# One-hot rows for the first expert block, a fixed expert order, row scaling on ScalarE and a resident norm row

## What is computed

```python
hn = rmsnorm(h, norm_ffn_w)
g_sel = argmax(hn @ router_group_w + b)                # one of 4 groups
top_l, top_i = top_k(e_logits of that group, 2)        # two of its 8 experts
weights = p_group * softmax(top_l)
ys = (silu(xb @ w_gate[e]) * (xb @ w_up[e])) @ w_down[e]   # per block of tokens of one expert
h = h + segment_sum(ys * buf_w, buf_tok)
out = rmsnorm(h, final_norm_w)
```

## Time and profile before

| | |
|---|---|
| median of 3 runs | 2898.2 us (2897.41 to 2901.9) |
| profiled execution | 2901.05 us |
| its span, first to last instruction | 2899.3 us |
| TensorE busy | 2523.1 us (87%) |
| VectorE busy | 917.7 us (32%) |
| ScalarE busy | 776.6 us (27%) |
| GpSimd busy | 171.6 us (6%) |
| DMA | 610.93 MB, mean 211 GB/s |

### The profile page before, as it was taken

The page is one execution under the profiler, slowest core; times in us unless marked ns, Lnnn a source line. Parts: engine busy times, 40 slices in busy tenths (PEclk is TensorE's granted clock), DMA queues, the critical chain, the costliest instruction groups (busy, mean ns, idle before and its releaser), DMA issues. The chain is left out here.

```text
span 2899.3 us, 39218 instructions
## 1 busy us (share of the span) xinstructions
PE 2523.1 (87%) x15509; PEld 1649.2 (57%) x15509; DVE 917.7 (32%) x1218; ACT 776.6 (27%) x958; POOL 171.6 (6%) x236
## 2 busy tenths in 40 slices
PE   5999999999999999998999995987777877877771
PEld 4888888887777777776788783332232223222220
DVE  3333333335554555554443224100010001000004
ACT  4444444433343334433222221111111111111111
POOL 0000000000000000000000004000000000000000
PEclk9999999999999999999899997999999999899995
DMA  4333333332222222233545326999999999999984
GB/s 141 102 101 101 101 101 101 101 102 71 76 74 69 70 74 75 74 81 112 163 137 187 105 73 241 395 407 410 402 413 410 411 406 401 394 409 406 398 338 192
DMA packets 315196, 610.93 MB, mean 211 GB/s; under 512 B 18910, under 2 KB 240474, under 8 KB 260698
## 3 DMA queue, kind: packets, MB, share of 16 engines
q1 hardware_dynamic: 303948, 568.03, 54.2%
q0 software_dynamic: 11152, 41.45, 4.0%
HBM read 585.82 MB, written 41.42 MB: 216 GB/s over the span
## 5 line engine op out<-in xcount | busy, mean ns | idle before, releaser
L1957 PE MATMUL bank<-ex_w_gate,ex_xt_sb 128*64 128x512 f32 x1024 | 492.4, 631 | 160.3 <-DMA ex_w_up<-in_expert_w_up_dram 145.6
L153 PE MATMUL in_z<-xn_hi,in_hi 128*128 128x512 f32 x1456 | 584.0, 401 | 21.4 <-DVE in_lo L185 21.4
L153 PE MATMUL in_z<-xn_lo,in_hi 128*128 128x512 f32 x1456 | 582.5, 400 | 0.0
L153 PE MATMUL in_z<-xn_hi,in_lo 128*128 128x512 f32 x1456 | 579.1, 398 | 0.0
L1959 PE MATMUL bank<-ex_w_up,ex_xt_sb 128*64 128x512 f32 x1024 | 495.5, 634 | 0.0
L1957 PEld LDWEIGHTS bank<-ex_w_gate,ex_xt_sb 128*64 128x64 f32 x1024 | 139.7, 145 | 479.0 <-issue 478.8
L185 DVE TENSOR_TENSOR in_lo<-in_raw,in_hi 128x2048 fp32r<-128x2048 f32 x123 | 292.5, 2378 | 312.6 <-ACT in_hi L180 192.2
L153 PEld LDWEIGHTS in_z<-xn_hi,in_hi 128*128 128x128 f32 x1456 | 274.3, 188 | 84.0 <-issue 21.5
L1925 DVE TENSOR_TENSOR ex_act_g<-bank,ex_sig 64x512 f32<-64x512 f32 x32 | 21.9, 684 | 935.5 <-ACT ex_sig L1901 935.5
L153 PEld LDWEIGHTS in_z<-xn_lo,in_hi 128*128 128x128 f32 x1456 | 274.3, 188 | 67.2 <-issue 10.8
L153 PEld LDWEIGHTS in_z<-xn_hi,in_lo 128*128 128x128 f32 x1456 | 274.0, 188 | 63.5 <-issue 5.0
(11 more groups left out here) (417 smaller groups left out, 2882.2 us busy)
## 6 DMA issues: line engine op xcount, KB each, us to landing
ex_w_gate<-in_expert_w_gate_dram SPq DMA_DIRECT2D x128, 1024.0 KB, 15.7
ex_w_up<-in_expert_w_up_dram SPq DMA_DIRECT2D x128, 1024.0 KB, 27.4
ex_w_down<-in_expert_w_down_dram SPq DMA_DIRECT2D x128, 1024.0 KB, 26.6
in_raw<-in_w_in_dram SPq DMA_DIRECT2D x91, 1024.0 KB, 5.7
in_raw<-in_w_out_dram SPq DMA_DIRECT2D x32, 512.0 KB, 4.7
in_raw<-in_w_branch_hg_dram SPq DMA_DIRECT2D x16, 512.0 KB, 5.2
in_raw<-in_w_branch_rw_dram SPq DMA_DIRECT2D x16, 512.0 KB, 6.2
mg_gates<-scratch_gate SPq DMA_DIRECT2D x16, 512.0 KB, 3.9
```

The costliest lines, as they stand in the source:

```text
L153: return pe.matmul(out, w[:, k, :], x[:, k, :], start=(n == 0), stop=(n == PASSES * KT - 1), skip_group_check=True)
L1957: pe.matmul(gate_up[low, :], x_t[u][:, k, :], w_gate[n][:, j, :], start=first, stop=last, skip_group_check=True)
```

## The change

1. **The first 32 blocks are experts 0 to 31 in order.** A first block of up to 64 tokens per expert has the number of the expert; what an expert has beyond 64 tokens follows in blocks from 32 on. `limits` no longer counts a first block, `blocks` and `ends` count the further ones, and a token's slot is 64 times its expert plus its rank, unless the rank is 64 or more (`late_e`). SyncE loads experts 1 to 30 by the loop's counter, without waiting for the tables; block 31 and later ones take their expert from `blk_expert`. The engines wait for `n_blocks` only.
2. **Block 0's rows** are not gathered and not transposed. `of_first[P, 4, 64]` is a one-hot matrix (token to slot of expert 0) times `rstd`; TensorE multiplies the transposed slice of `h` with it: for each of 16 column tiles and 4 token tiles, a stationary 128x128 piece of `h`, whose columns are four elements apart, against 64 moving columns (L1846 of the new kernel). This stands between the rank matmuls and the table.
3. **ScalarE scales the rows** and permutes them; GpSimd only stores them.
4. **The rows of odd blocks** are gathered into partitions 64 to 127 of one tile `ex_x[P, 2048]`, and `sig` and `act_g` share a tile; this makes room for a resident `final_norm_w` tile, which SyncE loads behind expert 0.
5. **Combine** has no such load and no wait for it. The last tile's last pass and store are in two halves.

```diff
+    made.done(ts(pre["slots"][:], ramp[:, 0:SLOTS], 1.0, None, ALU.mult))
+    made.done(ts(pre["expert_slot"][:], ramp[:, 0:N_EXPERTS], float(SLOTS), None, ALU.mult))
+    made.done(ts(pre["from_first"][:], ramp[:, 0:N_EXPERTS], float(SLOTS), -(SLOTS - 1) / 2.0, ALU.mult, ALU.add))
...
-    made.done(dve.memset(pre["limits"][:, 0:1], -1.0))
+    made.done(dve.memset(pre["limits"][:, 0:1], float(4 * T)))
...
+    keep["w_final"] = mem.sb("final_norm_rows", [P, D])
...
+    both = mem.sb("ex_x", [P, D])
+    keep["xg_both"], keep["xg"] = both, [both[SLOTS * s:SLOTS * s + SLOTS, :] for s in range(2)]
...
+        sp.dma_start(keep["w_final"][:], io["final_norm_w"].rearrange("(a d) -> a d", a=1).to_broadcast([P, D])
+                     ).then_inc(keep["router_in"], 16)
...
+        order.wait()
+        order.done(tt(in_first[:], m12[:, :, 0], rstd[:], ALU.mult))
 
         dve.wait_ge(pe_done, RANK_DONE)
+        order.done(tt(of_first[:], rank_ps[:, 0:TT, 0:1].to_broadcast([P, TT, SLOTS]),
+                      slots[:].rearrange("p (a s) -> p a s", a=1).to_broadcast([P, TT, SLOTS]), ALU.is_equal))
+        order.wait()
+        mark("first", tt(of_first[:], of_first[:], in_first[:].rearrange("p (t a) -> p t a", a=1).to_broadcast([P, TT, SLOTS]),
+                         ALU.mult))
         step(tt(over[:], rank_ps[:, TT, :].rearrange("p (e a) -> p e a", a=1).to_broadcast([P, E, PG]),
                 limits[:].rearrange("p (a g) -> p a g", a=1).to_broadcast([P, E, PG]), ALU.is_gt))
         step(dve.tensor_reduce(blocks[:], over[:], AX_X, ALU.add))
         step(dve.tensor_tensor_scan(ends[:], ones_e[:], blocks[:], 0.0, ALU.mult, ALU.add))
-        step(stt(start[:], ends[:], -(SLOTS - 1) / (2.0 * SLOTS), blocks[:], ALU.add, ALU.subtract))
-        step(stt(slot_e[:], start[:].rearrange("p (a e) -> p a e", a=1).to_broadcast([P, TT, E]), float(SLOTS),
-                 rank_ps[:, 0:TT, :], ALU.mult, ALU.add))
+        order.done(tt(pairs[:], ends[:, E - 1:E].to_broadcast([P, MAX_BLOCKS // 2]), evens[:], ALU.is_gt))
+        step(stt(start[:], ends[:], float(E - 1), blocks[:], ALU.add, ALU.subtract))
+        step(dve.tensor_reduce(total[:], pairs[:], AX_X, ALU.add))
+        mark("n_blocks", ts(keep["n_blocks"][:], total[0:1, :], 2.0, float(E), ALU.mult, ALU.add))
+        step(stt(start[:], start[:], float(SLOTS), expert_slot[:], ALU.mult, ALU.subtract))
+        all_t = lambda a: a[:].rearrange("p (a e) -> p a e", a=1).to_broadcast([P, TT, E])
+        step(stt(late_e[:], rank_ps[:, 0:TT, :], float(SLOTS), all_t(start), ALU.is_ge, ALU.mult))
+        step(tt(late_e[:], late_e[:], all_t(from_first), ALU.add))
+        step(tt(slot_e[:], late_e[:], rank_ps[:, 0:TT, :], ALU.add))
...
-        step(tt(pairs[:], ends[:, E - 1:E].to_broadcast([P, MAX_BLOCKS // 2]), evens[:], ALU.is_gt))
-        step(dve.tensor_reduce(total[:], pairs[:], AX_X, ALU.add))
-        order.done(ts(keep["n_blocks"][:], total[0:1, :], 2.0, None, ALU.mult))
...
+        order.done(dve.tensor_copy(keep["blk_expert"][:, 0:1], ramp[0:1, E - 1:E]))
         dve.wait_ge(pe_done, EXPERT_DONE)
-        mark("blocks", dve.tensor_copy(keep["blk_expert"][:], expert_ps[:, 0:MAX_BLOCKS + 2]))
+        mark("blocks", dve.tensor_copy(keep["blk_expert"][:, 1:MAX_BLOCKS - E + 2], expert_ps[:, 0:MAX_BLOCKS - E + 1]))
...
-        for s in range(2):
-            pool.memset(xg[s][:], 0.0).then_inc(zero_ready, 1)
-        after(pool, "rstd")
+        pool.wait_ge(zero_ready, 1)
+        pool.memset(keep["xg_both"][:], 0.0).then_inc(zero_ready, 1)
         for t in range(TT):
-            if t >= 2:
-                pool.wait_ge(hn_stored[t % 2], 16 * (t // 2))
-            pool.tensor_scalar(hn[t % 2][:].rearrange("s (n j p) -> s n p j", j=4, p=P),
-                               h[:, t, :].rearrange("s (n p j) -> s n p j", j=4, p=P), rstd[:, t:t + 1], None,
-                               ALU.mult).then_inc(hn_scaled, 1)
             pool.wait_ge(hn_scaled, t + 1)
             pool.dma_start(io["hn"][t * P:(t + 1) * P, :], hn[t % 2][:]).then_inc(hn_stored[t % 2], 16)
         for s in range(2):
...
         act.activation(tmp[:], rstd[:], ACT.Sqrt).then_inc(act_done, 1)
         for k in range(2, KT, 2):
             copy(k)
-        act.wait_ge(zero_ready, 3)
+        act.wait_ge(zero_ready, 2)
         act.wait_ge(lgt_done, KT // 2)
         act.activation(lg_t[low, :], lgt_ps[low, :], ACT.Copy).then_inc(lgt_read, 1)
+        after(act, "rstd")
+        for t in range(TT):
+            if t >= 2:
+                act.wait_ge(hn_stored[t % 2], 16 * (t // 2))
+            act.activation(hn[t % 2][:].rearrange("s (n j p) -> s n p j", j=4, p=P),
+                           h[:, t, :].rearrange("s (n p j) -> s n p j", j=4, p=P), ACT.Copy,
+                           scale=rstd[:, t:t + 1]).then_inc(hn_scaled, 1)
...
+        after(pe, "first")
+        by_slot = lambda b: b[:].rearrange("p (k s) -> p k s", s=SLOTS)
+        for g in range(2):
+            for k in range(8):
+                f = P * 4 * ((8 * g + k) // 4) + (8 * g + k) % 4
+                for t in range(TT):
+                    rows = h[:, t, :].rearrange("s (d j) -> s d j", j=4)[:, f // 4:f // 4 + P, f % 4]
+                    mm = pe.matmul(by_slot(bank[2 + g])[:, k, :], rows, of_first[:, t, :], start=(k == 0 and t == 0),
+                                   stop=(k == 7 and t == TT - 1), skip_group_check=True)
+            mm.then_inc(keep["x_turned"], 1)
...
-    sig, act_g, h_sb = (mem.sb("ex_" + n, [P, D_EXPERT]) for n in ("sig", "act_g", "h"))
+    sig, h_sb = (mem.sb("ex_" + n, [P, D_EXPERT]) for n in ("sig_gate", "h"))
+    act_g = sig
...
-        eng.wait_ge(keep["route_steps"], keep["route_at"]["blocks"])
+        eng.wait_ge(keep["route_steps"], keep["route_at"]["n_blocks"])
         return eng.value_load(keep["n_blocks"][:], min_val=N_EXPERTS, max_val=MAX_BLOCKS)
 
     @block.sync
     def _(sp):
-        def load(b, after):
-
-            e = bass.ds(sp.value_load(keep["blk_expert"][0:1, bass.ds(b, 1)], min_val=0, max_val=N_EXPERTS - 1), 1)
+        def load(b, e):
+
             for n in range(PAIRS):
-                wait_apart(sp, loads_passed, unit_used, UNITS * after + n + 1)
+                wait_apart(sp, loads_passed, unit_used, UNITS * b + UNITS + n + 1)
                 load_pair(sp, io, keep, e, n)
             for n in range(DC):
-                wait_apart(sp, loads_passed, unit_used, UNITS * after + PAIRS + n + 1)
+                wait_apart(sp, loads_passed, unit_used, UNITS * b + UNITS + PAIRS + n + 1)
                 load_down(sp, io, keep, e, n)
 
+        with sp.Fori(1, N_EXPERTS - 1) as b:
+            load(b, bass.ds(b, 1))
         n_blocks = blocks(sp)
-        with sp.Fori(0, n_blocks - 2, 2) as i:
-            for u in range(2):
-                load(i + u + 1, i + u + 2)
-        load(n_blocks - 1, n_blocks)
+        sp.wait_ge(keep["route_steps"], keep["route_at"]["blocks"])
+        with sp.Fori(N_EXPERTS - 1, n_blocks) as b:
+            load(b, bass.ds(sp.value_load(keep["blk_expert"][0:1, bass.ds(b - (N_EXPERTS - 1), 1)], min_val=0,
+                                          max_val=N_EXPERTS - 1), 1))
+        sp.wait_ge(keep["router_in"], 16 * 6)
...
-        for s in range(2):
-            fetch(s, keep["tok_table"][:, s:s + 1])
+        fetch(1, keep["tok_table"][:, 1:2])
...
-                    mm = pe.transpose(x_ps[g][:, k, :], xg[s][:, f:f + P], ident)
+                    mm = pe.transpose(x_ps[g][:, k, :], xg[s][:, f:f + P], (ident, ident_high)[s])
                 mm.then_inc(x_turned, 1)
 
-        turn_x(0, 16)
...
-                turn_x(v, 8 * i + 16 + 16 * u)
+                turn_x(v, 8 * i + 16)
...
+        pieces = [(t, slice(0, D)) for t in range(TT - 1)] + [(TT - 1, slice(0, D // 2)), (TT - 1, slice(D // 2, D))]
...
-            sp.dma_start(w_bc[:], io["final_norm_w"].rearrange("(a d) -> a d", a=1).to_broadcast([P, D])).then_inc(w_in_, 16)
-            for t in range(TT):
-                sp.wait_ge(finished, t + 1)
-                sp.dma_start(io["out"][0, t * P:(t + 1) * P, :], h[:, t, :]).then_inc(stored, 16)
-            sp.wait_ge(stored, 16 * TT)
+            for n, (t, part) in enumerate(pieces):
+                sp.wait_ge(finished, n + 1)
+                sp.dma_start(io["out"][0, t * P:(t + 1) * P, part], h[:, t, part]).then_inc(stored, 16)
+            sp.wait_ge(stored, 16 * len(pieces))
...
-                dve.scalar_tensor_tensor(h[:, t, :], h[:, t, :], rstd[:, c], w_bc[:], ALU.mult, ALU.mult).then_inc(finished, 1)
+                for part in (p for at, p in pieces if at == t):
+                    dve.scalar_tensor_tensor(h[:, t, part], h[:, t, part], rstd[:, c], w_bc[:, part], ALU.mult,
+                                             ALU.mult).then_inc(finished, 1)
 
             for t in range(TT):
                 add(t)
-                if t == 1:
-                    dve.wait_ge(w_in_, 16)
```

32 lines of the change are left out of this document (21 added, 11 removed).

## The result

The kernel after takes a median of 2903.7 us (2900.9 to 2910.0, 20 runs), the one before, timed beside it, 2897.1 us (2894.6 to 2901.9, 20 runs). The ratio is 1.0021, with a 95% interval of 1.0015 to 1.0028: slower by 4 to 8 us, at and just over the 0.2% that can be told from no change. The profiled execution of after took 2902.38 us, with a span of 2900.7. It is only 1.4 us longer in span than that of before, so the two profiles side by side account for less than the medians do, which differ by 6.7. That gap of some 5 us was the question of most experiments.

What follows compares the result with a forecast made beforehand. DMA was taken to bound the expert stage, delayed by block 0's first products. First place +11.4 and end -11.0 us gave +0.4, forecast 2898.6 us, range 2883 to 2910 (the forecast's own 2894 to 2903).

Steps and rivals of the forecast that it cites:

- The bound: Expert stage is a pipe filled by DMA; each microsecond block 0's first products move is one of the end.
- Slower: Outcome slower by over 0.2%: long strided stream, end not giving its 10 us, or stall staying; chance 0.19.
- rival B: One-hot stream: 16-byte stride makes loads 1.7 times as long, stream 49.8 us, total 2919; chance 0.13, partly or in full.
- end without its 10 us: Rival for the last phase: results' loads hold VectorE or the early row delays something; up to 2909, chance 0.04.
- VectorE's stall: Routing: 3.89 us lost beside GpSimd's scaling pass, counted as won with ScalarE scaling; +3.9 if it stays.
- Part 1: Path to the first product before: mask, ranks, table, VectorE steps, gather, transposes, copies; first product at 1806.13.
- The stream: Block 0's 64 one-hot matmuls on TensorE: 128 rows at the low clock, 29.3 us, lower bound 15.5.
- factor of 1.7: Strided against adjacent reading per element, 1.76 against 1.04 ns, from VectorE reductions; applied to TensorE's strided loads.
- Behind the stream: After the one-hot stream: table 1.95, VectorE steps 3.0, bare n_blocks load 1.16, copies 1.4, then 0.25 us.
- The first pair: Block 0's first pair of products, 6.9 us at the low clock (1806.13 to 1813.03), forecast unchanged.
- the first place: Path to block 0's first products, which delays expert 1's first load: +11.4 us, first product at 1817.5.
- The end: Last phase: resident norm row saves 10.06 us, halved last store 0.9; sum -11.0, between -9.5 and -12.

Runs made afterwards that it cites:

- gather_block0: The kernel after with block 0's rows gathered again, without the 64 one-hot matmuls and the passes for their mask: 2893.4 us, ratio 0.9985 to before.
- warm_stream: The kernel after with eleven useless 512-wide matmuls on TensorE before the wait for VectorE's mask: 2905.0 us, ratio 1.0030 to before.
- rows_low: After with the norm's row loaded in the last phase, last tile stored whole (2915.5 us), plus odd blocks' rows back in partitions 0 to 63: 2911.1 us.
- split_rows_low: gather_split with odd blocks' gathered rows back in partitions 0 to 63, router's transposes moved to make room: 2886.3 us, ratio 0.9957 to before.
- stream_adjacent: The kernel after with the one-hot matmuls' stationary operand read from adjacent columns of h (computes something else there): 2900.4 us.
- gather_split: After with block 0 gathered, GpSimd scaling two tiles and ScalarE two, the norm's row loaded after the stores: 2892.1 us, ratio 0.9980 to before.

## Why the forecast was close, and where it failed

**The bound.** Right: the delay of the first load of expert 1 was passed on to the end in full, in each of the kernels, within the scatter of the stage.

**The number.** 2903.7 us lies within 2883 to 2910, and 0.7 above the upper end of the forecast's own range, 2894 to 2903. The change was forecast at +0.4 us and measured at +6.7 and +4.8 by the medians, so the middle of the forecast missed, and it is the width of the range that took the result in. "Slower" had a chance of 0.19, for reasons of which none came true: no longer stream as in rival B, no end without its 10 us, no stall that stayed.

**VectorE's stall.** Right. The ranks are read 25.11 us after the first load of expert 0 instead of 29.02: the 3.9 us of the forecast. But Part 1 read the path of before wrongly where it goes from VectorE through the table to the gather: there the table was ready 2.7 us before the gather, and the last store, which landed 1.1 us ahead of it, closed the path. The sum is not touched, since it starts from the measured 1806.13. That ScalarE's passes are hidden was right for this kernel only. They took 3.8 to 3.9 us each, the upper end that I had named, though the view in L1785 reads adjacent elements and writes them 512 bytes apart, and is no strided read. Where the gather is needed early (gather_block0) the last store lands 2.3 us later than in before, and the stall's end brings nothing. This was not seen.

**The stream.** Its size was right, 30.1 us for 29.3, for a reason that was half right. At the low clock an adjacent load takes 0.215 us and a strided one 0.235 us, so the stride, not the clock, set the pace, and in the 2 us at the full clock (warm_stream) it was 0.23 as well. The sentence under rival B, that the stride may only forbid the gain of the full clock, is what the runs showed; the factor of 1.7 came from VectorE and did not carry over. On the rule cited there (the Trainium skill, SBUF — State Buffer, Door 1: The DMA port swizzle), of two hits on a 16-byte line for full speed: the warm stream agrees with it in sign, 0.235 us at the full clock against 0.121 for adjacent columns.

**Behind the stream.** The steps, the bare load of n_blocks (1.18 for 1.16) and the copies came as costed. The first product is 13.1 us later than in the profile of before, 12.1 with the longer trunk taken off, for 11.4 forecast; the stream's 0.8 is all of the difference.

**The first pair.** I took 6.9 us as unchanged from one profile. It was 5.2 to 6.4 us in the other thirteen profiles, 5.8 and 5.7 in the two others of before. Before's front is 57.6 on average of three profiles, not 58.7, so the first place costs 69.8 - 57.6 = 12.2 us instead of 11.4.

**The end.** 11.0 to 11.2 us for 11.0.

**What failed** is the step that reads "The shared tile of the gate and the other partitions for odd blocks' rows change no count of bytes; I cost them at nothing and allow 1 us on either side". The partitions cost 3.3 us by the profiles, 4 to 6 by the medians; the reason given for nothing, an unchanged count of bytes, did not hold. With it the sum is 12.2 - 11.1 + 3.3 = +4.4 us, which lies between the two measurements of after (+3.8 by a ratio of 1.0013, +6.1 by 1.0021). The forecast of +0.4 as the difference of two effects of 11 us was right in both effects and left out a third one in the stage of 1000 us, where 0.3% weigh as much as a third of either. The shared tile of the gate was not tried alone, since there is no room for two tiles beside the rest; but rows_low and split_rows_low keep it, and their stages, 1032.4 and 1028.7, lie about the 1030.6 to 1032.2 of before, so no cost of it shows.

## What to carry to other kernels

Where a long stage is bound by DMA, an edit of it is not free because its bytes are the same: here a new place for the gathered rows had a price of 0.3%, and with a scatter of several microseconds it takes medians of the parts undone one at a time to see it. Replacing a gather by one-hot products pays only if TensorE's stream is shorter than the gather's path, and the work that the queue holds behind it belongs in the middle of the stream (4.2 us here). When an engine is relieved of a job, look at what really closed the path: removing VectorE's stall brought nothing where the gather waited for the last store, which came no earlier from ScalarE.

## What the runs showed of the hardware

- TensorE's loads of 128 f32 columns 16 bytes apart follow one another every 0.235 us at the low clock, and nine of them every 0.23 us at the full one (warm_stream); those of adjacent columns every 0.215 us at the low one (stream_adjacent).
- A stream of such loads, adjacent or not, with 64 moving columns behind each and without a gap, did not raise the granted clock from 0.50 in 28 to 30 us; a clock that was full at its start fell 2 us into it.
- A ScalarE pass over 128x2048 that permutes the columns, with adjacent reads and writes 512 bytes apart, takes 3.8 to 3.9 us (after), an adjacent one 1.9.
- A store of 1 MB beside expert 0's loads lands 7 to 12 us after its issue (before, gather_block0, gather_split, after), one in the last phase after 3.9.
- Gathered rows in partitions 64 to 127 instead of 0 to 63, for every second block, made a stage bound by DMA 0.3% longer.
